# The triangular inverse of an RWKV-7 layer on Trainium2: 32x32 blocks on four array tiles in place of 64x64 on two

## The reference

```python
def wkv_scan(s0, r, decay, k, v, kk, a):
    def step(s, inp):
        r_t, w_t, k_t, v_t, kk_t, a_t = inp
        sa = jnp.einsum("bhij,bhj->bhi", s, -kk_t)
        s = (s * w_t[:, :, None, :] + sa[..., None] * (kk_t * a_t)[:, :, None, :]
             + v_t[..., None] * k_t[:, :, None, :])
        return s, jnp.einsum("bhij,bhj->bhi", s, r_t)
    ...
    s, o = lax.scan(step, s0, xs)
```

## Time and profile before

| | |
|---|---|
| median of 3 runs | 2350.82 us (2348.98 to 2351.67) |
| the profiled execution | 2344.9 us, its span 2343.3 us |
| TensorE busy | 2159.1 us, 92% of the span |
| VectorE, ScalarE, GpSimd busy | 39%, 27%, 14% |
| the RWKV stage's first middle starts | 145.42 us |
| the last pair's recurrence starts | 953.18 us |
| levels' stretch, pair 0 / 5 | 28.13 / 30.39 us |
| all six levels' stretches | 178.02 us |

### The profile page before, as it was taken

The page is one execution under the profiler, slowest core; times in us unless marked ns, Lnnn a source line. Parts: engine busy times, 40 slices in busy tenths (PEclk is TensorE's granted clock), DMA queues, the critical chain, the costliest instruction groups (busy, mean ns, idle before and its releaser), DMA issues. The chain is left out here.

```text
span 2343.3 us, 47109 instructions
## 1 busy us (share of the span) xinstructions
PE 2159.1 (92%) x20794; PEld 1416.1 (60%) x20794; DVE 911.4 (39%) x1765; ACT 634.3 (27%) x1433; POOL 319.2 (14%) x279
## 2 busy tenths in 40 slices
PE   7999999999999999997997999999898788589997
PEld 3577585775866857654554555555566555355664
DVE  3253462543634526323314313053322677522332
ACT  5321222223222223121214111121222566211111
POOL 0000020110201102020001032120010566101110
PEclk9999999999999999999989999999898899699998
DMA  7000010000100000007002021100002000546652
GB/s 254 30 20 11 10 40 19 29 21 10 31 29 29 12 19 30 21 15 280 1 27 104 27 84 65 65 10 9 28 27 72 1 1 1 190 179 226 210 194 92
DMA packets 52798, 147.84 MB, mean 63 GB/s; under 512 B 11459, under 2 KB 20995, under 8 KB 51316
## 3 DMA queue, kind: packets, MB, share of 16 engines
q1 hardware_dynamic: 42612, 103.97, 12.7%
q0 software_dynamic: 9984, 40.87, 4.9%
HBM read 123.58 MB, written 21.24 MB: 62 GB/s over the span
## 5 line engine op out<-in xcount | busy, mean ns | idle before, releaser
L755 PE MATMUL psum<-xT,rw_w 128*128 128x384 f32 (+1 forms) x1152 | 397.7, 484 | 2.8 <-PEq L169 2.8
L755 PEld LDWEIGHTS psum<-xT,rw_w 128*128 128x128 f32 x1152 | 206.1, 189 | 119.9 <-issue 9.4
L2014 PE MATMUL psum<-spare,xT 128*128 128x384 f32 (+1 forms) x432 | 143.3, 494 | 1.5 <-PEq L169 1.5
L2014 PE MATMUL psum<-kvq_w,xT 128*128 128x384 f32 (+1 forms) x432 | 140.6, 487 | 0.0
L1292 DVE SCALAR_TENSOR_TENSOR rwkv_xs<-psum,rwkv_pc,rwkv_xsc 128x64 f32<-128x64 f32 x90 | 25.6, 284 | 238.9 <-PE psum L968 238.9
L2014 PEld LDWEIGHTS psum<-spare,xT 128*128 128x128 f32 (+1 forms) x432 | 80.4, 187 | 62.7 <-issue 13.6
L2014 PEld LDWEIGHTS psum<-kvq_w,xT 128*128 128x128 f32 (+1 forms) x432 | 79.0, 184 | 61.3 <-issue 11.2
L723 POOL DMA_DIRECT2D out<-rwkv_s x6 | 5.7, 953 | 760.5 <-ACT rwkv_out_p L1118 760.5
L1097 ACT COPY rwkv_r_sb<-psum 128x64 f32<-128x64 f32 x96 | 20.4, 212 | 327.9 <-PE psum L948 296.2
L2416 PE MATMUL psum<-V,yT 128*128 128x512 f32 x192 | 105.2, 675 | 0.0
L2093 DVE TENSOR_REDUCE kvq_ss<-kvq_sq 128x6 f32<-128x384 f32 (+1 forms) x36 | 19.9, 552 | 201.8 <-ACT kvq_sq L2056 201.7
(11 more groups left out here) (437 smaller groups left out, 4051.0 us busy)
## 6 DMA issues: line engine op xcount, KB each, us to landing
xT<-in_cache_k SPq DMA_DIRECT2D x64, 384.0 KB, 3.8
samp_vp<-in_cache_v POOLq DMA_DIRECT2D x64, 384.0 KB, 4.5
rw_w<-in_w_in SPq DMA_DIRECT2D x28, 512.0 KB, 3.6
front_w<-in_mem_w_kv SPq DMA_DIRECT2D x2, 2048.0 KB, 14.5
x_rows<-in_x_p SPq DMA_DIRECT2D x8, 512.0 KB, 14.0
h<-in_x_p SPq DMA_DIRECT2D x8, 512.0 KB, 13.3
residual<-h POOLq DMA_DIRECT2D x8, 512.0 KB, 3.3
xT<-in_w_out SPq DMA_DIRECT2D x2, 1536.0 KB, 13.1
```

Source lines behind the costliest of these rows:

```text
L755: mm = pe.matmul(out, w[:, load % 2, k, :], xT[:, k, a:b], start=(k == 0), stop=(k == KC - 1))
L2014: mm = pe.matmul(bank[0:r, j % 6, 0:W], xT[:, k, n * P:n * P + r], w[i % 2][:, k, :], start=(k == 0), stop=(k == KC - 1))
```

## The change

The levels up to 16 are worked out on 32x32 blocks: each head's 64x64 matrix has two diagonal 32x32 blocks, so a chunk has four of them for the pair, one for each quarter of the partitions (`quarter`), and each matmul of a level takes one quarter. The matrices D, E and the masked products become half as wide (`ddq`, `eeq`, `mmq`, 32 columns a chunk in place of 64), and so do the DVE and ACT operations on them. The first blocks come from PE (`first_blocks` picks the diagonal blocks out of `am` by a matmul with the identity, which turns them too), DVE masks them, and `first_turn` makes the transpose. The level 32 goes: since the inverse of a block triangular matrix is made of the two blocks' inverses and one product of three, `cross_products` makes the first product of that, `place_blocks` puts the two inverses into the 64x64 result in PSUM by matmuls with the identity, and `place_cross` the product. Level 16 is turned now as well. ACT and DVE then copy half of the result each to `ee`, whose lower left blocks were set to zero once. The third `gated_turn` and `gated` of the pair before follow behind level 16, and `fill(p + 1, 0)` of the first step of the recurrence moves ahead of the matmul that reads `ee`.

The core of the diff:

```diff
-LEVELS = [2, 4, 8, 16, 32]
+LEVELS = [2, 4, 8, 16]
...
+        ddq = kkT[:, 0:NCHUNK * QB].rearrange("p (n t) -> p n t", t=QB)
+        eeq = kkT[:, NCHUNK * QB:2 * NCHUNK * QB].rearrange("p (n t) -> p n t", t=QB)
+        mmq = prev[:, 0:NCHUNK * QB].rearrange("p (n t) -> p n t", t=QB)
...
-            def first_inverse(p, g):
-                pe.wait_ge(e0_ready, NG * p + g + 1)
-                for u in range(4 if g < GROUPS else 1):
-                    for d in half:
-                        mm = turned(bank[d, g, u * CH:(u + 1) * CH], ee[d, 4 * g + u, :], d)
-                mm.then_inc(d0_turned, 1)
+            def first_blocks(p, g):
+                pe.wait_ge(am_ready, NFILL * p + min(2 * g + 2, NFILL))
+                for u, n in enumerate(range(NCHUNK)[group(g)]):
+                    for q, d in enumerate(quarter):
+                        mm = pe.matmul(level_bank(g)[d, u, :], am[d, n, 0, own_block(q)], ident[d, d], start=True, stop=True)
+                mm.then_inc(d0_mm, 1)
...
+            def block_products(p, lev, k, g):
+                if lev == 0:
+                    pe.wait_ge(t0_ready, NG * p + g + 1)
+                else:
+                    pe.wait_ge(d_ready, NLEV * p + before(k) + 1)
+                for u, n in enumerate(range(NCHUNK)[group(g)]):
+                    for q, d in enumerate(quarter):
+                        mm = pe.matmul(level_bank(g)[d, u, :], am[d, n, 0, own_block(q)], ddq[d, n, :], start=True, stop=True)
+                mm.then_inc(m_mm, 1)
...
+            def cross_products(p, k, g):
+                pe.wait_ge(d_ready, NLEV * p + k + 1)
+                for u, n in enumerate(range(NCHUNK)[group(g)]):
+                    for h in range(2):
+                        mm = pe.matmul(level_bank(g)[quarter[2 * h + 1], u, :], am[quarter[2 * h], n, 0, QB:CH], ddq[quarter[2 * h], n, :],
+                                       start=True, stop=True)
+                mm.then_inc(x_mm, 1)
+
+            def place_blocks(p, k, g):
+                pe.wait_ge(e_ready, NLEV * p + k + 1)
+                for u, n in enumerate(range(NCHUNK)[group(g)]):
+                    for q, d in enumerate(quarter):
+                        mm = pe.matmul(final_bank(g)[d, u, own_block(q)], ident[d, d], eeq[d, n, :], start=True, stop=True)
+                mm.then_inc(placed, 1)
...
-                pe.wait_ge(e_ready, NTURN * (p + 1))
-                pe.wait_ge(fin_ready, GROUPS * (p + 1))
+                for g in range(3):
+                    place_blocks(p, LAST_STEP + g, g)
+                place_cross(p, 0)
+                place_cross(p, 1)
+                place_blocks(p, LAST_STEP + 3, 3)
+                if p >= 1:
+                    gated_turn(p - 1, 2)
+                place_cross(p, 2)
+                place_cross(p, GROUPS - 1)
...
+                    if n == 0:
+                        fill(p + 1, 0)
+                    if n % 8 == 0:
+                        pe.wait_ge((fin_act, fin_dve)[n // 8], p + 1)
...
+                act.wait_ge(fin_mm, GROUPS * p + 2)
+                for h in range(2):
+                    nc.scalar.copy(ee[quarter[2 * h], 0:8, 0:QB], final_pair(0)[quarter[2 * h], :, 0:QB])
+                nc.scalar.copy(ee[:, 0:8, QB:CH], final_pair(0)[:, :, QB:CH]).then_inc(fin_act, 1)
```

More of the change, by code:

```diff
@@ L586, in rwkv_pairs @@
     half = [slice(0, HS), slice(HS, P)]
+    quarter = [slice(q * QB, (q + 1) * QB) for q in range(4)]
     with Stage(nc, "rwkv") as st:
@@ new lines, in block_updates, with block_turn @@
+            def block_updates(p, lev, k, g):
+                pe.wait_ge(m_ready, NLEV * p + k + 1)
+                if lev >= 1:
+                    pe.wait_ge(e_ready, NLEV * p + before(k) + 1)
+                for u, n in enumerate(range(NCHUNK)[group(g)]):
+                    for d in quarter:
+                        mm = pe.matmul(level_bank(g)[d, u, :], eeq[d, n, :], mmq[d, n, :], start=True, stop=True)
+                mm.then_inc(dm_mm, 1)
+            def block_turn(p, k, g):
+                pe.wait_ge(d_ready, NLEV * p + k + 1)
+                j, free = turn_place(k)
+                if free >= 0:
+                    pe.wait_ge(e_ready, NLEV * p + free + 1)
+                for u, n in enumerate(range(NCHUNK)[group(g)]):
+                    for d in quarter:
+                        mm = turned(turn_bank(j, g)[d, u, :], ddq[d, n, :], d)
+                mm.then_inc(e_turned, 1)
@@ L819, in gated_turn, with place_cross @@
+            def place_cross(p, g):
+                pe.wait_ge(placed, GROUPS * p + g // 2 * 2 + 2)
+                pe.wait_ge(cross_ready, GROUPS * p + g + 1)
+                for u, n in enumerate(range(NCHUNK)[group(g)]):
+                    for h in range(2):
+                        lower = quarter[2 * h + 1]
+                        mm = pe.matmul(final_bank(g)[quarter[2 * h], u, QB:CH], mmq[lower, n, :], eeq[lower, n, :], start=True, stop=True)
+                mm.then_inc(fin_mm, 1)
             def gated_turn(p, part):
@@ L861, in middle @@
                     for k, g in steps:
[L862 to L869, removed]
@@ L870, in middle @@
-                    for k, g in steps:
[L871 to L876, removed]
-                                    mm = pe.matmul(level_bank(g)[d, u, :], ee[d, n, :], mm_[d, n, :], start=True, stop=True)
-                                else:
-                                    mm = pe.matmul(level_bank(g)[d, u, :], mm_[d, n, :], ee[d, n, :], start=True, stop=True)
-                        mm.then_inc(dm_mm, 1)
@@ L881, in middle @@
[L881 to L889 removed]
+                        if lev == 0 and g == 3:
+                            first_turn(p, 3)
+                            first_turn(p, GROUPS)
@@ L912, in sample_part @@
                     pe.wait_ge(rs_ready, p + 1)
-                    for d in half:
-                        mm = pe.matmul(bank[d, 2, HS:2 * HS], ee[d, NPC, :], rs_sb[d, :], start=True, stop=True)
+                    for d in quarter:
+                        mm = pe.matmul(bank[d, 2, HS:2 * HS], ee_s[d, 0, :], rs_sb[d, :], start=True, stop=True)
                     mm.then_inc(sas_mm, 1)
@@ L963, in recurrence @@
                     mm.then_inc(sa_mm, 1)
-                    fill(p + 1, 3 * n)
+                    if n > 0:
+                        fill(p + 1, 3 * n)
                     fill(p + 1, 3 * n + 1)
@@ L1127, in _ @@
             link = Chain(dve, dve_chain)
+            for h in range(2):
+                nc.vector.memset(ee[quarter[2 * h + 1], :, 0:QB], 0.0)
             nc.vector.memset(dec[:, :, 0:1], 1.0)
```

113 lines of the change are left out of this document (71 added, 42 removed).

## The result

The changed kernel takes 2525.81 us (median of 4 runs, 2521.25 to 2532.25) against 2349.90 us (4 runs), 1.077 times as long (95% interval 1.075 to 1.078). Its profiled execution took 2524.82 us, 179.9 us more than that of before.

The account below looks back on a forecast made before the run. The levels were taken to be bound by TensorE's instruction supply, 256 per 3.7 us. 2344.9 + 149 (levels) + 6 (clock) = 2500 us, with the median 5.9 us higher 2506, rounded to 2505; range 2390 to 2545.

Parts of the forecast that it names:

- The mechanism: In the levels, TensorE gets 256 instructions per 3.7 us, whatever they do, and stands under "issue" 2 to 3 us between.
- Rival 1: In the levels, the next instruction packet is ordered earlier, so one costs 2.45 us; 2395 us in all; chance 0.08.
- Rival 2: In the levels, instruction supply does not bind; TensorE's and VectorE's work and hand-overs do; 2279 us; chance 0.12.
- Rival 3: In the levels, the four tiles don't work side by side; each record costs 29.1 ns; 2511 us; chance 0.05.
- the levels' term: Extra time in the levels' stretches from more TensorE instructions: +24.8 us for each of five pairs, +24.9 for pair 0, +149.
- (a): At the levels' entry: 1.8 us a pair deducted, as the stretch begins on average in the middle of a loop.
- (b): In the levels, one loop, the supply of 256 TensorE instructions, takes 3.7 us, bounds 3.45 and 3.9.
- The clock: TensorE's clock might fall to 1.2 GHz and slow the recurrence's first matmuls: +1 us a pair, bounds 0 and +3.
- The stretch ahead: Stretch ahead of the levels: some 1280 instructions, just not bound by supply; 0, bounds -1 and +1.5 us a pair.
- The end copies: Copies of each half of ee at the levels' end: taken at nothing; uncovered, 1.2 us a pair, 7 us in all.
- The sum: Whole kernel: profiled 2344.9 us plus 149 for the levels and 6 for the clock, 2500; median 5.9 above, so 2506.
- the two buffers of the prediction: TensorE's instruction supply: two buffers of 256 instructions; entering one starts the other's refill, and crossing into that must wait.

Follow-up runs that it names:

- count_block: Kernel before plus 460 one-column 32x32 matmuls a pair, all in a row behind the first level's products; 2510.46 us against 2344.54, ratio 1.070.
- wide: Changed kernel with each level product's and update's moving operand reaching to the end of its four-chunk group, same instruction count; 2525.15 us.
- merged: Changed kernel with block placements done by one 128-column matmul per group of four chunks instead of four with 32; 2497.10 us.
- after_dve: Changed kernel with the levels' turns done by 18 VectorE transposes of 32x32 blocks instead of 264 TensorE matmuls a pair; 2431.59 us.
- count64: Kernel before plus one one-column matmul on 64x64 tiles ahead of each level matmul, so no tile shape changes; 2532.52 us (one run).

## Where the prediction was right, and where not

It said 2505 us, 2390 to 2545; measured were 2525.81.

**The mechanism** held: 217 packets, as foretold; standstills under "issue" once in 256 instructions; loops instead of an even pace; VectorE and ScalarE, busy 12.3 and 9.8 us a pair, not in the way. The run count_block shows it without any of the change: 460 tiny matmuls a pair, against the 480 more that the change puts into the levels, cost 166 us. Some sizes that were named did not hold. The stretches were to take 53 to 57 us and took 55.95 to 59.15. The standstills were to last 2 to 3 us and lasted 1.5 to 2.5 (less where a burst holds gated turns), since a burst takes 1.8 us and not 1 to 1.5: records are 8 to 9 ns apart only in the first burst and 14 ns behind it, at the halved clock. Loops were to take 3.5 to 3.9 us and took 3.3 to 4.2.

**Rival 1** (2.45 us per packet) fell: each packet starts when its burst has begun, and no whole loop takes less than 3.3 us. **Rival 2** (the supply does not bind) fell with the standstills. With it falls, for this kernel, what the Trainium skill (Runtime: NRT & Kernel Launch, Instruction fetch mechanics) says of the crossing of a block, that it is mostly hidden: the page gives TensorE room for 2048 instructions, and the trace has a standstill of 1.5 us or more behind nearly each 256 of the narrow matmuls' instructions. **Rival 3** (29 ns per record) is refuted by the bursts: 128 records on four row tiles that write to one PSUM bank, each to its own 32 partitions, take 1.14 us in count_block. The Trainium skill's rule behind it (TensorEngine Tiling (Array Packing), Gotcha 1: PSUM Pressure) says that row tiles cannot use one bank at the same time; 9 ns per record, a third of the 29.1 ns of the earlier trace rows, speaks against a cost of that kind here.

**The size of the levels' term** was 21 us too small (149 against 170.3). (a) "Less about half a loop (1.8 us), since the stretch begins on average in the middle of one" was wrong and is 10.8 of the 21 us. The stretch is entered with nothing in store: TensorE stands for 1.2 to 2.5 us within the first 1.1 us of each of the six, 2.24 us in pair 0:

```profile
165.04 0.56 PEld L854 LDWEIGHTS psum<-rwkv_dd,rwkv_am 32*32 32x32 f32 x51
167.84 0.48 PEld L854 LDWEIGHTS psum<-rwkv_dd,rwkv_am 32*32 32x32 f32 x45 [2.24 <-issue]
```

With the deduction left out the forecast would have been 160. (b) The loop was taken at 3.7 us. The 80 loops from the first full burst to the last start of one in the six stretches take 3.77 us on average (3.70 in pair 0, 3.82 in pair 3), which over 14.8 + 5 x 15.3 = 91.3 packets is 6.4 us more. (c) The last 4 us are the slow entry of (a), where a stretch's first packet or so costs more than a loop.

The gated turns are not among the parts, although at 1.2 GHz their 32 loads take 1.78 us, against 1.01 us at the full clock:

```profile
741.90 0.93 PEld L753 LDWEIGHTS psum<-base,rwkv_dd 32*32 32x32 f32 x61 [1.96 <-issue]
742.89 1.78 PEld L753 LDWEIGHTS psum<-base,rwkv_o_all 64*64 64x64 f32 x32
744.79 0.60 PEld L854 LDWEIGHTS psum<-rwkv_dd,rwkv_am 32*32 32x32 f32 x35
746.01 0.62 PEld L854 LDWEIGHTS psum<-rwkv_dd,rwkv_am 32*32 32x32 f32 x40 [0.62 <-issue]
```

The burst that holds them lasts 3.49 us, the standstill behind it shrinks to 0.62 us, and the loop takes 4.11 us; the other one of pair 3 takes 3.85 us, and loops without such turns up to 4.22 us. More work inside a burst is paid by the standstill, as in the run wide.

**The clock** fell, and stayed low into the recurrence, as allowed for. Taken was 1 us a pair, bounds 0 and 3; it was about 2. The time from a recurrence's start to the next middle sums up to 519.2 us over five pairs, against 509.3 before, and behind the start of the sixth recurrence the kernel takes 3.1 us more: 13.0 us for six. The first 3.40 us of the recurrences ran at 0.50 to 0.60 with TensorE busy throughout, which at half the clock is up to 1.7 us lost, and in pair 3 the next 3.40 us still show 0.67. The run merged, where five of six start at 1.00, is shorter by 1.7 us a pair on average over the first five. How far the clock falls inside the levels does not matter, as the run wide shows.

**The stretch ahead** was taken at 0, bounds -1 and +1.5 us a pair; it is -0.65 us. **The end copies** were taken at nothing, rightly: in pair 3 the last placements start at 765.14 us and the recurrence at 765.49, and TensorE's only idle time ahead of the first reader of `ee` (L1039) is put down to another copy of ScalarE's (L1183), 3.1 us in the whole run.

**The sum** came nearer than its terms. They add up to 155 us, and the profiled executions differ by 179.9. Of these 25 us, 5 were given back by luck: the median was to lie 5.9 us above the profiled execution, as before, and lay 1.0 us above it.

What stays open: why a loop takes 3.64 us. The runs show that it hangs neither on the matmuls' columns nor on waits for data, that a packet starts 1.0 to 1.15 us behind the start of a burst, and that the next burst follows 2.4 to 2.7 us behind the packet (count_block). They don't show when the packet is ordered, what either part is spent on, or how many buffers there are: the two buffers of the prediction are a reading that fits.

## What to carry to other kernels

Count TensorE's instructions before cutting matmuls into smaller ones. A float32 matmul here leaves four records, two weight loads and two matmuls. This stretch already ran at 14.5 ns per instruction; there, more and smaller matmuls made it slower, whatever the array could do, and each matmul removed from the changed levels gave back 51 ns (merged, 14.7 us for 288) to 61 ns (after_dve, 96.7 us for 1584). Look for standstills put down to "issue" that lie 256 instructions apart, and take the gain on the other side: fewer and larger matmuls, work moved to an engine with time left, then the wait that the shorter stretch lays bare.

## What was not expected of the hardware

- A change of tile shape between two matmuls costs 0.27 us at the halved clock (0.54 us for the way there and back, 2760 times) and 0.17 us at the full one, and a change between the transposing and the multiplying form 0.26 and 0.16 us. The changed kernel keeps its phases whole and so pays this only a few times per pair.
- TensorE's clock fell to 1.2 GHz in a stretch in which it works about half of each loop. From 165.04 to 169.50 us of the changed kernel it was busy 2.04 of 4.46 us at 1.00; in the 46 us from 174.70 on it was 0.50 throughout:

```profile
165.04:169.50 4.46, 2.04 (x200) 1.81 (x186) 1.39 (x7) 0.62 (x3) 0.00 (x0) 1.00 0.03 7
...
174.70:220.90 46.20, 25.01 (x1573) 23.29 (x1573) 7.38 (x27) 6.57 (x25) 0.00 (x0) 0.50 0.02 5
```

- In count64 it fell in one pair of six, behind a stretch with waits of about 1 us, and then stayed low for most of 86 us in which TensorE was busy all the time. The profile shows no reason for its length.
